# Attention scores on stacked high and low query halves, split once per chunk, in a one-core encoder layer

## What is computed

```python
h = _rms(x, norm1_g)
q, k, v, c = jnp.split(h @ w_in, ...)        # 8 query heads, 2 key/value heads, 64 wide
q = _rms(q, q_norm_g);  k = _rms(k, k_norm_g)
s = jnp.einsum("bnqkgd,bnskd->bnkgqs", qb, kb) * (hd ** -0.5)   # 128 queries against a band of 384 keys
s = jnp.where(valid, s + bias, NEG_INF)      # ALiBi, window of 128
p = jax.nn.softmax(jnp.concatenate([s, sink_col], -1), -1)[..., :-1]
o = jnp.einsum("bnkgqs,bnskd->bnqkgd", p, vb)
u = silu(layernorm(dwconv31(a * sigmoid(gate))))                # the other half of c
x = x + jnp.concatenate([o, u], -1) @ w_out
x = x + (silu(dwconv3(h2 @ w_gate)) * (h2 @ w_up)) @ w_down     # h2 = rms(x), 2816 wide
```

## Time and profile before

| | |
|---|---|
| median of three runs | 2586.32 us (2582.92 to 2586.57) |
| the profiled execution, its own time | 2584.95 us |
| its span, first to last instruction | 2583.2 us |
| TensorE matmuls | 2558.4 us busy (99%), 12927 |
| VectorE, ScalarE, GpSimd busy | 72%, 49%, 7% |
| granted TensorE clock, mean | 0.999 |
| scores groups | 80, between 111 and 1313 us |

### The profile page before, as it was taken

How to read it: one execution, slowest core, us unless ns; L and a number is a source line. 1 busy time by engine, 2 the same in 40 slices (tenths; PEclk the granted TensorE clock), 3 DMA queues, 4 the chain that set the end, 5 groups by cost and what they waited for, 6 DMA issues and landing times. The chain is left out here.

```text
span 2583.2 us, 35531 instructions
## 1 busy us (share of the span) xinstructions
PE 2558.4 (99%) x12927; PEld 2287.9 (89%) x12927; DVE 1861.0 (72%) x3099; ACT 1266.6 (49%) x2179; POOL 184.7 (7%) x316
## 2 busy tenths in 40 slices
PE   8999999999999999999999999999999999999999
PEld 6877777788878887888888999999999999999999
DVE  4775658887888697969793687657667875765765
ACT  6345554468337843693563344335334443533532
POOL 0110021101011101110101100000000100000000
PEclk9999999999999999999999999999999999999999
DMA  9967778834564465446438542222213522221212
GB/s 346 351 226 237 263 276 336 289 117 164 191 215 141 141 245 216 163 159 247 169 121 350 190 146 66 65 62 70 63 61 119 171 63 65 66 65 60 69 58 70
DMA packets 139757, 419.11 MB, mean 162 GB/s; under 512 B 24160, under 2 KB 38880, under 8 KB 122944
## 3 DMA queue, kind: packets, MB, share of 16 engines
q1 hardware_dynamic: 113632, 317.93, 36.4%
q0 software_dynamic: 25952, 98.92, 10.0%
HBM read 328.01 MB, written 88.77 MB: 161 GB/s over the span
## 5 line engine op out<-in xcount | busy, mean ns | idle before, releaser
L1477 ACT ACTIVATE part_hi<-part_raw 128x512 fp32r<-128x512 f32 x396 | 247.6, 627 | 387.7 <-DMA part_raw<-w_pass_t 158.2
L2222 PE MATMUL bank<-hw_hi,weights 128*128 128x462 f32 (+3 forms) x1408 | 420.8, 373 | 0.0
L1751 DVE SCALAR_TENSOR_TENSOR cc<-win,par,cc 128x512 f32<-128x512 f32 x600 | 408.2, 744 | 0.0
L2382 PE MATMUL bank<-mid,part_hi 128*128 128x414 f32 x1408 | 376.7, 348 | 2.4 <-DVE mid L1986 2.0
L1930 DVE TENSOR_TENSOR part_lo<-part_raw,part_hi 128x512 fp32r<-128x512 f32 x396 | 270.8, 688 | 136.3 <-ACT part_hi L1477 130.8
L2173 PE MATMUL bank<-h_hi,weights 128*128 128x512 f32 x1104 | 355.2, 395 | 0.0
L2222 PEld LDWEIGHTS bank<-hw_hi,weights 128*128 128x128 f32 x1408 | 264.8, 188 | 37.4 <-issue 12.2
L2382 PEld LDWEIGHTS bank<-mid,part_hi 128*128 128x128 f32 x1408 | 263.3, 188 | 4.2 <-DVE mid L1986 3.4
L2222 PE MATMUL bank<-hw_lo,weights 128*128 128x464 f32 (+3 forms) x704 | 259.3, 368 | 0.0
L2173 PEld LDWEIGHTS bank<-h_hi,weights 128*128 128x128 f32 x1104 | 207.8, 188 | 51.6 <-issue 5.3
L2368 PE MATMUL bank<-T_hi,part_hi 128*128 128x414 f32 (+1 forms) x704 | 246.0, 349 | 0.4 <-DVE e L1954 0.4
(11 more groups left out here) (220 smaller groups left out, 4298.2 us busy)
## 6 DMA issues: line engine op xcount, KB each, us to landing
weights<-weight_scratch SPq DMA_DIRECT2D x88, 1024.0 KB, 6.0
wraw<-w_ffn_t SPq DMA_DIRECT2D x88, 512.0 KB, 3.5
part_raw<-w_ffn_t SPq DMA_DIRECT2D x176, 256.0 KB, 2.7
weight_scratch<-weights POOLq DMA_DIRECT2D x22, 1024.0 KB, 7.9
wraw<-w_down_t SPq DMA_DIRECT2D x44, 512.0 KB, 3.7
part_raw<-w_pass_t SPq DMA_DIRECT2D x88, 256.0 KB, 2.6
cat_hi<-cat_scratch SPq DMA_DIRECT2D x10, 1024.0 KB, 6.8
cat_lo<-cat_scratch SPq DMA_DIRECT2D x10, 1024.0 KB, 8.8
```

Source lines behind the costliest of these rows:

```text
L1477: nc.scalar.activation(p_hi[k % HI_RING][:], p_raw[part_of(k)][:], ACT.Copy).then_inc(s_whi, 1)
L1751: nc.vector.scalar_tensor_tensor(acc, win[i][:, tap:tap + TB], w_tap, acc, ALU.mult, ALU.add).then_inc(s_cv, 1)
L2222: mm = nc.tensor.matmul(out, l[:, k, :], r[:, k, cols], start=(k == 0 and j == 0), stop=(k == KT - 1 and j == 2))
L2382: mm = nc.tensor.matmul(bank[BANK_Y[n % 4]][:, 0:TP], l[:, (deep * o + t) % KH, :], mid2[:, t, part, i, :], start=(t == 0 and z == 0), sto ...
```

## The change

`store_qk`'s tiles are split before they are stored. Per tile, ScalarE makes a high part (`qk_split_high`, into one of two new buffers `qk_hi`), VectorE turns `qk` in place into the low part (`qk_split_low`), and GpSimd stores both: two DMAs of 256 KB a tile in the place of one. The keys and queries of chunk 0 go this way too. `load_k` reads the band four times a chunk, high and low, each into both partition halves (`k_hi_twice`, `k_lo_twice`); `load_q` makes four DMAs of 128 KB a block, so that for each head the high queries lie in partitions 0 to 63 and the low ones in 64 to 127 of one tile, `q_pair`, of which there is one buffer and no longer two. `scores` then makes two matmuls of 128 rows a head, `q_pair` x `k_hi_twice` and `q_pair` x `k_lo_twice`: (high + low) x high and (high + low) x low, four in all. The product low x low, which was left out, is now in the sum. The per-block splits on ScalarE and VectorE are gone; their number, 5 + 20, is that of the new ones. Line numbers of the changed kernel are smaller, by 26 at the projection's matmuls.

Chunk 0's first block moves from slot 16 to 20, and most tables of the order are new. The row pitch of the windows `hw_hi`, `hw_lo` and of `mid` falls from 512 columns to 480. A new wait: `qk_split_high` of tile M waits until both stores of tile M-2 have landed.

```diff
-ATTN_AT = {0: (16, 9), 1: (56, 11), 2: (99, 9), 3: (136, 11), 4: (178, 9)}
-CONV_AT = {0: (12, 45), 1: (56, 84), 2: (93, 125), 3: (139, 169), 4: (183, 212)}
-NORM1_AT = {0: (5, 6, 7), 1: (5, 5, 7), 2: (5, 5, 8), 3: (4, 5, 6)}
-XS_AT = (2, 6, 7, 9)
-EXP_AT = (3, 4, 4, 5)
+ATTN_AT = {0: (20, 9), 1: (56, 10), 2: (97, 10), 3: (137, 11), 4: (179, 9)}
+CONV_AT = {0: (12, 41), 1: (56, 84), 2: (93, 123), 3: (140, 167), 4: (182, 210)}
+NORM1_AT = {0: (4, 6, 8), 1: (4, 5, 7), 2: (4, 6, 8), 3: (4, 5, 6)}
+XS_AT = (4, 6, 8, 9)
+EXP_AT = (2, 3, 4, 5)
 DENOM_AT = 5
 NORMALISE_AT = (6, 7)
 TRANSPOSE_AT = (7, 7, 7, 8, 8, 8)
 VALUES_AT = 9
-ACT_FIRST = ('scale_copy', 'copy_t', 'k_high', 'attn_q_high')
-ACT_EARLY = ('ln_scale', 'copy_t', 'attn_q_high')
-DVE_FIRST = ('ln_centre', 'ln_add2', 'norm2', 'denom', 'ln_low', 'ln_apply', 'k_low')
-DVE_EARLY = ('bias', 'attn_q_low', 'norm_h', 'ln_add', 'qk_norm', 'ln_apply')
-LN_STEPS = {0: (0, 0, 0, 1, 1, 2, 4, 5, 5, 5), 1: (1, 2, 2, 2, 2, 3, 3, 4, 4, 5), 2: (1, 2, 2, 3, 3, 4, 4, 6, 9, 9), 3: (0, 1, 1, 3, 5, 6, 6, 7, 7, 8), 4: (0, 1, 1, 2, 2, 2, 2, 3, 3, 3)}
+ACT_FIRST = ('scale_copy', 'ln_swish', 'ln_scale', 'attn_q_high', 'qk_split')
+ACT_EARLY = ('ln_scale', 'copy_t')
+DVE_FIRST = ('ln_centre', 'ln_add2', 'qk_norm', 'qk_split', 'denom', 'ln_low', 'bias', 'norm_h')
+DVE_EARLY = ('ln_add', 'ln_apply', 'k_low', 'norm_h', 'qk_norm', 'bias')
+LN_STEPS = {0: (0, 0, 0, 1, 1, 2, 4, 5, 6, 6), 1: (1, 2, 2, 2, 2, 3, 3, 4, 4, 5), 2: (1, 2, 3, 4, 4, 5, 5, 7, 10, 10), 3: (1, 2, 2, 3, 5, 6, 6, 7, 8, 9), 4: (0, 1, 1, 2, 2, 2, 2, 3, 4, 4)}
...
         DVE_SIDE[_b + 11 + _m].insert(0, ("qk_norm", _c, _m))
-        POOL_SIDE[_b + 12 + _m].append(("qk_store", _c, _m))
+        ACT_SIDE[_b + 11 + _m].append(("qk_split", _c, _m))
+        DVE_SIDE[_b + 12 + _m].append(("qk_split", _c, _m))
+        POOL_SIDE[_b + 13 + _m].append(("qk_store", _c, _m))
...
     if _n == 0:
-        if _c > 0:
-            POOL_SIDE[_b - 2].append(("load_k", _c))
+        POOL_SIDE[_b - 2].append(("load_k", _c))
         POOL_SIDE[_b + 1].append(("load_v", _c))
-        ACT_SIDE[_b - (2 if _c == 0 else 1)].append(("k_high", _c))
-        DVE_SIDE[_b - (2 if _c == 0 else 1)].append(("k_low", _c))
-    if _N > 0:
-        POOL_SIDE[_b - 4].append(("load_q", _c, _n))
-    ACT_SIDE[_b - (2 if _n else 1)].append(("attn_q_high", _N))
-    DVE_SIDE[_b - (2 if _n else 1)].append(("attn_q_low", _N))
+    POOL_SIDE[_b - (4 if _N else 2)].append(("load_q", _c, _n))
...
-ROOM = (7.6, 6.9)
-WORK = {"norm_h": 2.0, "h_low": 1.6, "qk_norm": 1.0, "qk_inverse": 2.3, "qk_low": 0.9, "bias": 1.55, "denom": 0.4, "k_low": 1.4, "attn_q_low": 1.0, "attn_low": 0.9,
+ROOM = (7.1, 7.0)
+WORK = {"norm_h": 2.0, "h_low": 1.6, "qk_norm": 1.0, "qk_inverse": 2.3, "qk_low": 0.9, "bias": 1.55, "denom": 0.4, "qk_split": 0.7, "attn_low": 0.9,
...
-        q_d = dram("q_scratch", (AT, P, TOKENS))
-        k_d = dram("k_scratch", (P, TOKENS))
+        q_d = dram("q_scratch", (2, AT, P, TOKENS))
+        k_d = dram("k_scratch", (2, P, TOKENS))
...
-        M_PITCH, H_PITCH = pitch(TC), pitch(TH)
+        M_PITCH, H_PITCH = -(-TC // 32) * 32, -(-TH // 32) * 32
+        QK_BYTES = 4 * (TB * (NORMED + 9) + up(PICK_COLS) + NORMED * P)
...
+            ("q_pair", [P, KV_HEADS, AT, P], F32R), ("vw", [P, BLOCKS + 2, KV_W], F32), ("bias", [P, BAND], F32), ("win0", [P, TB + 2 * HALO], F32),
             ("win1", [P, TB + 2 * HALO], F32), ("cc", [P, CT, TB], F32),
-            ("attn_hi", [P, AT, P], F32), ("attn_lo", [P, AT, P], F32), ("qt_hi", [P, AT, P], F32R),
-            ("kw_hi", [P, TB + 2 * P], F32R))
+            ("attn_hi", [P, AT, P], F32), ("attn_lo", [P, AT, P], F32),
+            ("k_hi_twice", [P, KV_HEADS, TB + 2 * P], F32R), ("k_lo_twice", [P, KV_HEADS, TB + 2 * P], F32R))
...
-                pool.wait_ge(s_qn, NORMED * c + m + 1)
-                dst = k_d if m == 0 else q_d[m - 1]
-                pool.dma_start(dst[:, TB * c:TB * (c + 1)], qk[m]).then_inc(s_qst[m], 16)
+                M = NORMED * c + m
+                pool.wait_ge(s_alq, M + 1)
+                for part, src in enumerate((qk_hi[M % 2][:].bitcast(F32), qk[m])):
+                    dst = k_d[part] if m == 0 else q_d[part, m - 1]
+                    pool.dma_start(dst[:, TB * c:TB * (c + 1)], src).then_inc(s_qst[m], 16)
...
-                pool.wait_ge(s_qst[0], 16 * (c + 1 if c in (0, CHUNKS - 1) else c + 2))
-                pool.dma_start(kw[:, P * n0:P * n1], k_d[:, P * (t0 + n0):P * (t0 + n1)]).then_inc(s_kl, 16)
+                pool.wait_ge(s_qst[0], 32 * (c + 1 if c in (0, CHUNKS - 1) else c + 2))
+                for part in range(2):
+                    src = k_d[part].rearrange("(g d) n -> d g n", g=KV_HEADS)[:, :, P * (t0 + n0):P * (t0 + n1)]
+                    for half in range(2):
+                        rows = slice(HEAD_DIM * half, HEAD_DIM * (half + 1))
+                        pool.dma_start(k_twice[part][rows, :, P * n0:P * n1].bitcast(F32), src).then_inc(s_kl, 16)
...
-                if N >= 2:
-                    pool.wait_ge(s_qk, GROUP * (N - 1))
+                if N >= 1:
+                    pool.wait_ge(s_qk, GROUP * N)
                 for m in range(1, NORMED):
-                    pool.wait_ge(s_qst[m], 16 * (c + 1))
-                pool.dma_start(qt[N % 2][:], q_d.rearrange("t p n -> p t n")[:, :, P * N:P * (N + 1)]) \
-                    .then_inc(s_ql[N % 2], 16)
+                    pool.wait_ge(s_qst[m], 32 * (c + 1))
+                for part in range(2):
+                    for g in range(KV_HEADS):
+                        rows = slice(HEAD_DIM * g, HEAD_DIM * (g + 1))
+                        pool.dma_start(q_pair[HEAD_DIM * part:HEAD_DIM * (part + 1), g].bitcast(F32),
+                                       q_d[part].rearrange("t p n -> p t n")[rows, :, P * N:P * (N + 1)]).then_inc(s_ql, 16)
...
+            def qk_split_high(c, m):
+                M = NORMED * c + m
+                act.wait_ge(s_qn, M + 1)
+                if M >= 2:
+                    act.wait_ge(s_qst[(M - 2) % NORMED], 32 * ((M - 2) // NORMED + 1))
+                nc.scalar.activation(qk_hi[M % 2][:], qk[m], ACT.Copy).then_inc(s_ahq, 1)
...
+            def qk_split_low(c, m):
+                M = NORMED * c + m
+                dve.wait_ge(s_ahq, M + 1)
+                nc.vector.tensor_tensor(qk[m].bitcast(F32R), qk[m], qk_hi[M % 2][:].bitcast(F32), ALU.subtract) \
+                  .then_inc(s_alq, 1)
...
-                    pe.wait_ge(s_alq, splits_before(N) + 1)
-                if t > 0:
+                    pe.wait_ge(s_ql, 64 * (N + 1))
+                    if n == 0:
+                        pe.wait_ge(s_kl, 64 * (c + 1))
+                else:
                     pe.wait_ge(s_sb, HEADS * N + KV_HEADS * t)
-                parts = ((qt_hi, kw_hi), (qt_hi, kw_lo), (qt_lo[N % 2], kw_hi))
-                for i, (q, k) in enumerate(parts):
-                    for g in range(KV_HEADS):
-                        rows = slice(HEAD_DIM * g, HEAD_DIM * (g + 1))
-                        mm = nc.tensor.matmul(bank[SCORE[g]][:, P * ks[0]:P * (ks[-1] + 1)], q[rows, t, :],
-                                              k[rows, P * (n + ks[0]):P * (n + ks[-1] + 1)], start=(i == 0),
-                                              stop=(i == len(parts) - 1))
+                for g in range(KV_HEADS):
+                    for i, k in enumerate(k_twice):
+                        mm = nc.tensor.matmul(bank[SCORE[g]][:, P * ks[0]:P * (ks[-1] + 1)], q_pair[:, g, t, :],
+                                              k[:, g, P * (n + ks[0]):P * (n + ks[-1] + 1)], start=(i == 0), stop=(i == 1))
                 mm.then_inc(s_qk, 1)
```

More of the change, by code:

```diff
@@ L167 @@
 T_SEQ = {t: i for i, t in enumerate(T_LIST)}
-def splits_before(N):
-    return N + N // BLOCKS + 1
 PE_SIDE = {n: [] for n in range(SLOTS + 1)}
@@ L624, in encoder_layer @@
         xs, xt = [xs0, xs1], [xt0, xt1]
-        qk_all, q_inv, q_root, v_raw, rs1, vb, pick, spread, q_sq0, q_sq1 = run(
+        qk_all, q_inv, q_root, v_raw, rs1, vb, pick, spread, q_sq0, q_sq1, *qk_hi = run(
             R_HW, ("qk", [P, NORMED, TB], F32),
@@ L635, in encoder_layer @@
         R_ATTN = R_SIDE + 4 * 4 * TB
-        s0, s1, q0, q1, kw, vw, bias, win0, win1, cc, ah, al, qt_hi, kw_hi = run(
+        s0, s1, q_pair, vw, bias, win0, win1, cc, ah, al, *k_twice = run(
             R_ATTN, ("S0", [P, GROUP, BAND], F32), ("S1", [P, GROUP, BAND], F32),
-            ("qt0", [P, AT, P], F32), ("qt1", [P, AT, P], F32), ("kw", [P, TB + 2 * P], F32),
-            ("vw", [P, BLOCKS + 2, KV_W], F32), ("bias", [P, BAND], F32), ("win0", [P, TB + 2 * HALO], F32),
+            ("q_pair", [P, KV_HEADS, AT, P], F32R), ("vw", [P, BLOCKS + 2, KV_W], F32), ("bias", [P, BAND], F32), ("win0", [P, TB + 2 * HALO], F32),
             ("win1", [P, TB + 2 * HALO], F32), ("cc", [P, CT, TB], F32),
```

(30 more changed lines are left out.)

35 lines of the change are left out of this document (3 added, 32 removed).

## The result

The changed kernel takes 2603.93 us (median of five runs, 2598.58 to 2610.23) against 2582.92 of the kernel before beside it: a ratio of 1.0082, 95% interval 1.0069 to 1.0095. It is some 21 us slower where 9 us were forecast to be won. The profiled execution of after took 2600.23 us, its span is 2598.4.

A forecast was written before the change was run, and what follows sets the result against it. TensorE's instruction stream was taken to bound the kernel: 17 us less stream plus 8 us of stalls gave -9, from 2584.95 to 2576, plus 1.4 for the median: 2577 us. Own range 2572 to 2582; 8 in 10, 2565 to 2588.

The forecast's parts named there:

- What bounds the kernel, and the scores group: TensorE's instruction stream sets the end; a 384-column scores group falls from 0.93 to 0.70 us, read start to start.
- the 17 of the sum: Over 80 scores groups on TensorE, the stream falls from 69.5 to 52.6 us, 17 us shorter.
- Groups behind values: Ten scores groups right behind a block's values share the change-over; they cost 0.72 us now, 0.55 for 256 columns.
- The Trainium skill's rule on contractions of 64: Scores on TensorE: row tiling gains up to a factor of two, so by that alone the change would lose.
- Splits and row pitch at nothing: The 25 splits on ScalarE and VectorE cost nothing extra; the 480-column pitch at most 6 us either way, taken as 0.
- Stalls: 8 us, between 0 and 20: TensorE stalls from the high split's new wait for store landings: 8 us in all, between 0 and 20.
- The two places that were worked through: Chunk 0 to 1: stalls of 2.4 and 2.0 us; chunk 2 to 3: about 4 us before block 2's transposes.
- The bank's 2.0 us near 113: Chunk 0 to 1: TensorE's tile waits 2.0 us more for its bank, behind the fourth split and read-out.
- I charge nothing there: No stall for chunk 1 to 2, within half a us of the need, nor chunks 3 and 4, softmax further off.
- slower by the waits: VectorE, blocked on ScalarE's split, falls behind with the bias; TensorE waits at scores groups: 26 us, 2595; chance 0.06.
- The single-buffered query tile of another rival: Query tile landing late, first due in slot 20; one example for stalls of 14 to 20 us, 2585; chance 0.15.
- DMA: hidden: GpSimd's 25 more stores and 77 more loads, 60 us of issuing; query loads hidden if landing stays near 5 to 8 us.

The follow-up runs named there:

- Experiment 1: Kernel before with only the scores changed to four 128-row matmuls a group on the old operands, leaving out the right sums: 2567.50 us, ratio 0.9942.
- experiment 3: Changed kernel with four buffers for the high parts in place of two, so a split waits for tile M-4's stores: 2583.62 us, ratio 1.0006.
- experiment 7: Changed kernel with four buffers and, in chunk 1, the last token squares, root and norm's transposes one slot later: 2577.08 us, ratio 0.9974 against the kernel before.

## Why the prediction was wrong

*What bounds the kernel, and the scores group: right.* The step from starts and not from busy times gave 0.70, 0.71 was measured, and alone the scores bring 15.0 us (12 to 18) for the 17 of the sum. Groups behind values gain hardly anything, as forecast: 0.72 less 0.70 was 0.02, and 1.06 less 1.04 is what the rows show, as entering from the values' half-width output costs what it did. The Trainium skill's rule on contractions of 64 ("TensorEngine Tiling (Array Packing)", Performance Considerations; the words "up to 2×" stand in its Overview) would, taken alone, have made the change slower. Experiment 1 was faster: the pairs do run side by side, in 0.17, but six in pairs took 0.93 with their change-over, and four full ones 0.72.

*Splits and row pitch at nothing:* the pitch is 0 to 4 us by the times, about 2 by the spacing. The splits' own time was not isolated.

*"Stalls: 8 us, between 0 and 20": this term failed.* TensorE waited for 22 us more than before and lost up to 10 more to the clock. Two buffers cost 20 us against four. The two places that were worked through hold in part: at 95.6 TensorE waits 2.4 us for `h_low` (2.4 forecast), and at 301 3.2 us for the division (4 forecast):

```profile
98.40 0.79 PE L2147 MATMUL bank<-h_hi,weights 128*128 128x512 f32 x1 [2.39 <-DVE h_lo L1647]
...
304.67 1.53 PE L2282 MATMUL bank<-ident,S 128*128 128x128 f32 x12 [3.21 <-ACT S L1337]
```

The first agrees partly by luck: the keys' stores were out by 85.7 and not 90, took 10 us to land and not 7.6, and TensorE wanted the piece at 95.8 and not 98.4; the three errors cancel. The second came as worked out. The bank's 2.0 us near 113 did not come; 1.6 on the spreading operand came at 101.

What failed is the sentence "I charge nothing there" for chunks 1, 3 and 4. It followed the softmax alone. At 381 it was a copy of transposes that stood behind the split (4.5), at 420 the operand of the output projection (3.5, where the kernel before had 1.6; with four buffers 3.1 stay, so this one is not the split's doing), and at 531 the bias, at the end of the chain over four queues of experiment 3 (6.8). A landing was taken at 5.4 to 7.6 us from the earlier trace rows and was 15 at chunk 4. And nothing was charged for the clock: three of the four low stretches of after stand behind these uncharged waits.

The rival "slower by the waits" (26 us of stalls, 2595) came closest and was given 0.06; the way that it names, VectorE late with the bias, holds for 6.8 of the 22 us; "VectorE is 72% busy" was no argument against it, because what counts in an ordered queue is not how busy the engine is but what stands behind the blocked instruction. The single-buffered query tile of another rival cost 1.5 us once, at 139, and nothing with four buffers.

*"DMA: hidden": wrong, though it doesn't show in after itself.* With the landing waits gone, the key loads ahead of the token loads are the next cost, about 6.5 us: 2583.6 against 2577.1.

*Sum.* The kernel with four buffers and the later norm lies at 2577.1, 6.6 under before; the late token loads add 6.5, and the two buffers 20 more. That 6.6 and not 15 is won there lies in waits that stay. Against the profiled execution of experiment 1 (span 2566.8, waits 21.7 us, clock 0.999), that of experiment 7 has 5.7 us more of TensorE's waits and a span longer by 8.8; with four buffers alone it is 9.8 of waits, some 3 by a clock of 0.998, and 15.0; in after 22.1 of waits, up to 10 by the clock, and 31.6. The pitch's 2 us fit into what is left of the first two; the rest, up to 1 us, is open.

## What to carry over

Where a change puts a wait for a DMA's landing into an ordered queue, walk every place where it stands, not the tightest two, and list all that is queued behind it, on its engine and on those that wait for it in turn; a spare buffer or two that keeps the wait from being reached may be worth more than the change. Charge extra transfers to whoever else loads in those microseconds, and test one cause with the other removed: one delay can keep another from arising, as the late key loads of the changed kernel did.

## What the runs showed of the hardware

- Stretches at the lower clock stood behind TensorE's stalls of 2.4, 3.5, 4.5 and 6.8 us in after, of 3.1 and 6.0 with four buffers and of 1.9 in the kernel before. None stood behind the one of 3.2 in after that ends at 304.7, nor behind those of 2.0 in experiment 7. The length of a stall alone did not tell.
- 1 MB of loads ahead in the queues took a 512 KB load from 7.8 to 16.2 us.
- With each query store going from 128 partitions into two separate ranges of 64 rows of DRAM, three were issued, and then GpSimd stood for 18.5 us; the kernel took 2666.8 us for 2583.6. The edit also changed the rows' spacing in DRAM and the loads, and which of these does it was not taken apart.
- A group behind matmuls with a 64-column output starts 0.28 before its second matmul; between full-width ones 0.17.
